# Expert passes of 32 tokens: u rows by slot, v rows by token, summed in four column strips

## The reference, cut to what matters

```
q = (tb @ w_q).reshape(blk, 8 heads, 2 halves, 128)
s = einsum('thsk,hsnk->thsn', q, sub_keys)            # 128 scores per head and half
sv, si = top_k(s, 16)                                 # 16 best of each half
cand = sv[:, :, 0, :, None] + sv[:, :, 1, None, :]    # 256 pairs, 16 best of them
idx = si0 * 128 + si1 ; g = softmax(best 16)
act = gelu(einsum('thkd,td->thk', u_emb[idx], tb))    # 128 experts per token (8 heads x 16)
out = einsum('thk,thkd->td', g * act, v_emb[idx])
```

## Time and profile before

| | |
|---|---|
| three timed runs | 2709.21, 2710.64 (median), 2720.2 us |
| profiled execution | 2708.6 us, span 2706.6 us |
| granted PE clock, mean | 0.908 of full speed |
| busy: PE, DVE, POOL, ACT | 79%, 65%, 40%, 24% |
| DMA queue 0 (POOL's) | 570.46 MB, 52.7% of 16 engines |
| first gather, third gather, last gather | 1160.45, 1171.86, 2680.22 us |

### The profile page before, as it was taken

How to read it: one execution, slowest core, us unless ns; L and a number is a source line. 1 busy time by engine, 2 the same in 40 slices (tenths; PEclk the granted TensorE clock), 3 DMA queues, 4 the chain that set the end, 5 groups by cost and what they waited for, 6 DMA issues and landing times.

```text
span 2706.6 us, 34195 instructions
## 1 busy us (share of the span) xinstructions
PE 2130.6 (79%) x9927; PEld 1409.1 (52%) x9927; DVE 1767.8 (65%) x4439; ACT 657.1 (24%) x1597; POOL 1091.2 (40%) x822
## 2 busy tenths in 40 slices
PE   6988899999988898986777677766776676668776
PEld 6987778889977898952222223222322222223222
DVE  5887721143288434158787778777877787778785
ACT  4334300132255224321111111111111111111112
POOL 2553224365433342344444344434443443344342
PEclk9999967799998999999989898989989998898898
DMA  3220023222311232279999999999999999899997
GB/s 140 80 77 1 1 79 139 102 77 86 109 63 47 75 113 71 85 296 391 407 363 362 363 412 360 371 371 396 362 364 372 401 373 359 355 400 360 374 381 287
DMA packets 101508, 664.75 MB, mean 246 GB/s; under 512 B 11744, under 2 KB 12000, under 8 KB 29056
## 3 DMA queue, kind: packets, MB, share of 16 engines
q0 software_dynamic: 78336, 570.46, 52.7%
q1 hardware_dynamic: 20160, 71.92, 7.9%
q10 hardware_dynamic: 2880, 20.97, 2.0%
HBM read 650.38 MB, written 12.14 MB: 245 GB/s over the span
## 4 chain that ended last, share of the span: by engine, by line
DVE 33%; PE 25%; issue 24%; DMA 10%; POOL 4%; ACT 3%; DVEq 1%; POOLq 0%; SPq 0%; ACTq 0%
PE ps L404 12%; DMA s_r<-in_uv,s_gidx 9%; DVE s_r L1768 7%; PE ps L788 5%; DVE s_r L1380 4%; POOL s_r_rounded L1178 3%; DVE s_h L1768 2%; PE ps L641 2%; ACT s_gth L1134 1%; DVE s_r L1712 1%; PE ps L653 1%; DVE s_g L1773 1%; DVE s_g L1776 1%; DVE s_g L1772 1%; DVE s_g L1774 1%
## 5 line engine op out<-in xcount | busy, mean ns | idle before, releaser
L788 PE MATMUL ps<-s_r 128*128 128x512 f32 x1632 | 789.4, 632 | 236.5 <-ACT s_r L1141 235.6
L404 PE MATMUL ps<-s_r_rounded 128*128 128x272 f32 x5760 | 766.9, 296 | 35.7 <-POOL s_r_rounded L1178 10.6
L404 PEld LDWEIGHTS ps<-s_r_rounded 128*128 128x128 f32 x5760 | 753.4, 195 | 46.5 <-issue 28.2
L1331 POOL DMA_INDIRECT s_r<-in_uv,s_gidx x408 | 488.9, 1198 | 531.3 <-PE ps L788 441.5
L788 PEld LDWEIGHTS ps<-s_r 128*128 128x128 f32 x1632 | 309.6, 199 | 709.5 <-ACT s_r L1141 388.0
L1768 DVE CUSTOM_DVE_ANT_0 s_r<-s_r 128x1024 f32<-128x1024 f32 x408 | 486.9, 1222 | 59.6 <-DMA s_r<-in_uv,s_gidx 56.6
L1178 POOL TENSOR_TENSOR s_r_rounded<-s_r,s_r_rounded 128x1024 fp32r<-128x1024 f32 x120 | 305.5, 2547 | 469.6 <-ACT s_r_rounded L815 469.6
L788 PE MATMUL ps<-s_h,s_r 128*128 128x512 f32 x544 | 298.0, 698 | 208.6 <-ACT s_r L1141 208.6
L788 PEld LDWEIGHTS ps<-s_h,s_r 128*128 128x128 f32 x544 | 115.7, 224 | 385.9 <-ACT s_r L1141 252.2
L1134 ACT ACTIVATE s_gth<-s_g 128x2 f32<-128x2 f32 x272 | 55.4, 204 | 1036.8 <-DVE s_g L1774 1036.8
L1331 POOL DMA_INDIRECT s_h<-in_uv,s_gidx x136 | 156.1, 1148 | 344.5 <-PE ps L788 320.5
(11 more groups left out here) (242 smaller groups left out, 1932.2 us busy)
## 6 DMA issues: line engine op xcount, KB each, us to landing
s_r<-in_wstream SPq DMA_DIRECT2D x120, 512.0 KB, 3.3
s_h<-in_sample_h_in ACTq DMA_DIRECT2D x8, 1024.0 KB, 5.0
out_sample_h_out<-s_h ACTq DMA_DIRECT2D x8, 1024.0 KB, 3.9
s_r<-in_uv,s_gidx POOLq DMA_INDIRECT x408, 10.2
s_r<-in_x SPq DMA_DIRECT2D x4, 544.0 KB, 6.8
s_r<-in_x SPq DMA_DIRECT2D x1, 2176.0 KB, 8.4
s_h<-in_uv,s_gidx POOLq DMA_INDIRECT x136, 9.0
out_y_prompt<-s_r SPq DMA_DIRECT2D x4, 512.0 KB, 9.9
```

The lines of the kernel that those rows point to most:

```text
L404: last = pe.matmul(ps[:, 2 * p + h, 0:HALF], fr(wp[:, k, :]), fr(xp[:, k, h * HALF:(h + 1) * HALF]), start=start and k == 0 and t == 0, st ...
L788: last = pe.matmul(ps[:, h, :], diag[:, s % 4, :], ring[s % RING][:, D_MODEL + 512 * h:D_MODEL + 512 * (h + 1)], start=s == 0, stop=s == S ...
L1331: pool.indirect_dma_start(ring[sl % RING], None, a["uv"], bass.IndirectOffsetOnAxis(ap=gidx[:, j, s:s + 1], axis=0)).then_inc(gath[sl % RI ...
```

## The change

The expert part is laid out anew, and its hardware loops are gone.

- The table is split into `u` and `v`, each with rows of 4 KB. A pass (17 of them) now takes 32 tokens and all eight heads: the tokens stand four times on the partitions, once for each pair of heads, so partition 32q + t is token t with heads 2q and 2q + 1. The last pass is that of the sample tokens, and no longer a special case.
- u rows are gathered by slot (32 gathers of 128 rows, 512 KB each). v rows are gathered by token: the 32 x 32 blocks of the index tile are transposed, so that one gather brings the 128 v rows of one token (32 gathers of 512 KB). Each kind has a ring of 8 tiles of 4 KB per partition. POOL issues v of pass g and u of pass g + 1 in turns.
- gelu and the slot weights are computed once per pass on 128 x 32 elements. The weights are transposed and copied into every 32nd column of a zeroed tile `ZB`, so that the stationary operand of token t is 32 columns wide with only column t filled.
- PE takes v rows in groups of four tokens. Each of the four goes to another strip of 32 output columns; ACT copies the four partial sums out (`empty`), and PE adds them with the constant `sel` (`total`). v ring slots come free four at a time.
- The queries are ordered so that four units give one score set, which PE computes at once for all passes with 32-column matmuls (`scores`, 68 matmuls, four times). DVE's second routing of pass 0 needs the last of them.
- SP copies the token rows of each pass four times into a double buffer `tbg`.

```diff
-            def gathers(it, j):
-                pool.wait_ge(idx_ready, it * 2 + (j + 1))
...
-                        pool.wait_ge(slot_free, it * SLOTS + (sl - RING + 1))
-
-                        pool.nop(nofuse=True)
-                    pool.indirect_dma_start(ring[sl % RING], None, a["uv"],
-                                            bass.IndirectOffsetOnAxis(ap=gidx[:, j, s:s + 1], axis=0)
-                                            ).then_inc(gath[sl % RING], 16)
+            pool.wait_ge(unit_done, U_WQ)
+            pool.memset(ZB, 0.0).then_inc(zb_set, 1)
+
+            def gather_u(g, s):
+
+                n = g * SLOTS + s
+                if s % TOPK == 0:
+                    pool.wait_ge(idx_ready, 2 * g + s // TOPK + 1)
+                if n == 2:
+                    pool.wait_ge(unit_done, UNITS)
+                if n >= RING:
+                    pool.wait_ge(u_free, n - RING + 1)
+                pool.nop(nofuse=True)
+                pool.indirect_dma_start(uring[n % RING], None, a["u"],
+                                        bass.IndirectOffsetOnAxis(ap=gidx[:, g % 2, s:s + 1], axis=0)
+                                        ).then_inc(u_in[n % RING], 16)
+
+            def gather_v(g, t):
+
+                n = g * GT + t
+                if t == 0:
+                    pool.wait_ge(idxT_ready, g + 1)
+                if n >= RING:
+                    pool.wait_ge(v_free, (n - RING) // 4 + 1)
+                pool.nop(nofuse=True)
+                pool.indirect_dma_start(vring[n % RING], None, a["v"],
+                                        bass.IndirectOffsetOnAxis(ap=gidxT[:, g % 3, t:t + 1], axis=0)
+                                        ).then_inc(v_in[n % RING], 16)
...
-            gathers(0, 0)
-            gathers(0, 1)
-            with pool.Fori(1, ITERS) as it:
-                gathers(it, 0)
-                gathers(it, 1)
+            for s in range(SLOTS):
+                gather_u(0, s)
+            for g in range(GROUPS):
+                for t in range(GT):
+                    gather_v(g, t)
+                    if g + 1 < GROUPS:
+                        gather_u(g + 1, t)
...
+            def values(g):
+
+                bank = 4 * (g % 2)
+                pe.wait_ge(w_ready, g + 1)
+                if g >= 2:
+                    pe.wait_ge(evac_done, g - 1)
+                for quad in range(GT // 4):
+                    if g and quad == 3:
+                        total(g - 1)
+                    for c in range(4):
+                        n = g * GT + quad * 4 + c
+                        pe.wait_ge(v_in[n % RING], (n // RING + 1) * 16)
                     for h in range(2):
...
+                        for c in range(4):
+                            t = quad * 4 + c
+                            last = pe.matmul(ps[GT * c:GT * (c + 1), bank + h, :], ZB[:, g % 2, 31 * t + 31:31 * t + 63],
+                                             vring[(g * GT + t) % RING][:, 512 * h:512 * (h + 1)],
+                                             start=quad == 0, stop=quad == GT // 4 - 1)
+                    last.then_inc(v_free, 1)
...
+            def dot(g, s):
+
+                n = g * SLOTS + s
+                dve.wait_ge(u_in[n % RING], (n // RING + 1) * 16)
+                u = uring[n % RING]
+                dve.tensor_tensor_reduce(out=u, in0=u, in1=tbg[:, g % 2, :], scale=1.0, scalar=0.0, op0=ALU.mult,
+                                         op1=ALU.add, accum_out=act_z[:, s:s + 1]).then_inc(u_free, 1)
...
+            for g in range(GROUPS):
+                dve.wait_ge(tb_full[g % 2], 64 * (g // 2 + 1))
+                for s in range(SLOTS):
+                    if g + 1 < GROUPS:
+                        for j in range(2):
+                            if s == 11 * j + 2:
+                                route_keys(g + 1, j, 0)
...
+                    dot(g, s)
+                slot_weights(g)
```

More of the change, by code:

```diff
@@ L743, in _ @@
             pe.wait_ge(ld_late, 32)
[L745 to L761, removed]
+            def scores(i):
+                pe.wait_ge(q_ready, 4 * (i + 1))
+                if i:
+                    pe.wait_ge(sc_ready, i)
+                for g in range(GROUPS):
+                    for q in range(4):
+                        hs = (2 * q + i // 2) * 2 + i % 2
+                        out = ps[GT * q:GT * (q + 1), 4 + g // 4, (g % 4) * NKEYS:(g % 4 + 1) * NKEYS] if g < GROUPS - 1 \
+                            else ps[GT * q:GT * (q + 1), i, 512 - NKEYS:512]
+                        last = pe.matmul(out, qs[:, q, GT * g:GT * (g + 1)], keys[:, hs, :], start=True, stop=True)
+                last.then_inc(sc_mm, 1)
@@ L793, in _ @@
-            experts(0)
-            with pe.Fori(1, ITERS) as it:
-                experts(it)
-            pe.wait_ge(flushed, ITERS)
-            for h in range(2):
-                last = pe.matmul(ps[0:DEC, 2 + h, :], cc("sel"), X2T[:, TILES - 1, 512 * h:512 * (h + 1)],
-                                 start=True, stop=True)
-            last.then_inc(fin_mm, 1)
+            for i in range(HS // RINGW):
+                for j in range(RINGW):
+                    n = i * RINGW + j
+                    if n >= 2:
+                        pe.wait_ge(q_ready, n - 1)
+                    unit(U_WQ + n, j, j % 2, hn_parts, blocks=(hn_ready, KT) if n == 0 else None)
+                    if i and j == 0:
+                        scores(i - 1)
@@ L804, in _ @@
+            pe.wait_ge(sc_ready, 5)
+            for g in range(GROUPS):
+                values(g)
+            total(GROUPS - 1)
         @block.scalar
@@ L1158, in _ @@
-            squares = SC[:, 0:2, :].rearrange("p a b -> p (a b)")
-            softmax_exp(1)
-            experts(0)
-            with act.Fori(1, ITERS - 1) as it:
-                experts(it)
-            experts(ITERS - 1, True)
-            act.wait_ge(flushed, ITERS + 1)
-            token_norms(NCH, TILES, TILES, squares)
+            for n in range(HS):
+                keep_query(n)
+                if n >= RINGW and n % RINGW == 1:
+                    keep_scores(n // RINGW - 1)
+                if n == 2 * RINGW + 3:
+                    softmax_exp(0)
@@ new lines, in gelu_tanh @@
+            def gelu_tanh(g):
+                act.wait_ge(gl_in, g + 1)
+                act.activation(gth[:], g3[:], ACT.Tanh, scale=GELU_S).then_inc(gl_th, 1)
+            softmax_exp(1)
+            for g in range(GROUPS):
+                if g + 1 < GROUPS:
+                    softmax_exp(2 * g + 2)
+                if g >= 2:
+                    empty(g - 2)
+                if g + 1 < GROUPS:
+                    softmax_exp(2 * g + 3)
+                if g >= 5 and g % 4 == 1:
+                    token_norm((g - 5) // 4)
+                gelu_tanh(g)
```

359 lines of the change are left out of this document (152 added, 207 removed).

## The result

The changed kernel takes 2779.41 us (median of 4 runs, 2770.43 to 2799.22); the kernel before takes 2709.93 beside it. The ratio is 1.026, with an interval of 1.020 to 1.032: slower, by 0.6 of what was predicted (4.2%). The profiled execution took 2781.3 us with a span of 2779.5.

The account below looks back on a forecast made before the run. Experts were read as DMA-bound, with POOL bounding after the change: first dot 1187, pass 0 to 1237, 16 x 95.3 to 2762, last pass to 2805, ending at span 2823; predicted 2825 us (4.2% slower), range 2665 to 2930.

Parts of the forecast that it names:

- the choice on which all hung: POOL, experts: a gather of half the bytes still costs 0.94 us; if cost went with bytes, low end 49 us.
- the mean of a gather: POOL, experts: 1.19 us plus 0.30 between two, so 64 gathers cost 95.3 us a pass.
- bounds on both sides: POOL's pass: 79.7 us with DVE never in the way, 109 us at the high end.
- The last pass: End of the experts: 32 v gathers alone, 40 + 3 = 43 us.
- the loop of v buffers: Wait for v slots: landing 4.2 us plus 2.0 on PE, hidden behind eight issues of 11.9 us; costs nothing.
- The front end: Before the experts' passes: score sets 5 us each, first dot at 1187 against 1176.69, 10 us lost; first pass 50 us.
- the rivals, the first: Experts: DMA sets the pace as POOL's cost per gather falls; 87 us a pass, 2680 us; chance 0.19.
- DMA's share: Experts: DMA engines' share forecast near 0.85, at 350 GB/s.
- The forecast's own range: Whole kernel: POOL at 91 to 100 us a pass, 2765 to 2890 us; chance 0.59.
- Rival 2: Experts: 4 KB rows cost DMA the loose stretch's 48.1 ns per KB, 101 + 1.3 us a pass, 2935; chance 0.12.
- rival 3: Experts: PE becomes the bound, strips not overlapping and clock falling; 115 us a pass, 3155 us; chance 0.05.
- the turn of the loop: Old expert loop: DVE's 5.68 us standstill goes 15 times, 85 us in all, but off the path once POOL sets the pace.

Follow-up runs that it names:

- shorter holds: Changed kernel with each dot taken over 128 columns for 1024, same gathers and bytes: 2671.64 us (one run), 86.12 us a pass.
- short dots: Changed kernel with 2 KB rows gathered for 4 KB and dots over 128 columns, both together: 2573.36 us (one run), 80.98 us a pass.

## Why the prediction came out as it did

Direction and mechanism were right, and each stands on an experiment of its own.

POOL sets the pace: shown by half the bytes, which did not help, and by shorter holds, which did. That a half-size gather costs POOL the same 0.94 us was the choice on which all hung: shown, down to rows of 2 KB (0.961 us in the mean with short dots). The split alone makes an iteration of the old kernel 5 us longer, though there waits for PE have a part in it.

The term that was mis-sized is the mean of a gather, 1.19 us forecast and 1.121 measured (1.128 in the 16 passes). It makes a pass 91.7 us and not 95.3; 0.4 us of waits for buffers, which I had at nothing, come on top. So a pass was 92.08, and 16 passes 51 us less than forecast. The argument was that the share of gathers that meet a dot would stay. It did: 61% of the gathers took under 0.97 us before, 59% now. But how much of the dot is left when they meet it did not: 0.246 us over 0.94 in the mean then, 0.181 now. A gather that starts when a slot comes free and one that starts 0.30 us behind the last fall differently into the dots, and the half-row kernel (1.182) and the split one (1.086) show that this moves by itself. I had bounds on both sides and took the old mean; the rows of before hold nothing that gives 1.12.

The last pass went the other way: 43 us forecast, 54.4 measured. I had put the loop of v buffers at 4.2 us of landing and 2.0 of PE, against eight issues. In that pass there are no u gathers between, so four issues are 5 us; landing was 6.4; and a group took PE 3.64 us, on the lower clock level that I had named only as the other case. The groups then follow 7 us apart:

```profile
2709.34 3.64 PE L810 MATMUL ps<-s_r 128*32 128x512 f32 x16 [7.89 <-DMA s_r<-in_v,s_gidxT]
...
2715.91 3.64 PE L810 MATMUL ps<-s_r 128*32 128x512 f32 x16 [2.93 <-DMA s_r<-in_v,s_gidxT]
...
2723.68 3.64 PE L810 MATMUL ps<-s_r 128*32 128x512 f32 x16 [4.13 <-DMA s_r<-in_v,s_gidxT]
```

With the token rows in PSUM the last pass took 56.5 us, and 44.8 with 16 buffers, so the ring was the cause. This error and that of the gathers' mean have opposite signs, and the forecast came 11 us nearer by it.

The front end was close. Score sets took 3.92 us for 5, the first dot started at 1180.79 for 1187, and the first pass went its 50 us and a little (1232.4 for 1237):

```profile
1164.39 3.92 PE L768 MATMUL ps<-s_r 128*32 128x128 f32 x136 [0.71 <-ACT s_r L1115]
...
1180.79 1.19 DVE L1777 CUSTOM_DVE_ANT_0 s_h<-s_h 128x1024 f32<-128x1024 f32 x1
```

Together: -5 (pass stage starts earlier), -51 (passes), +11 (last pass), +1 (end), -44 of 2823 to 2779.5.

Of the rivals, the first had its floor right: once the holds are gone a pass is 86.1 us, and I had put DMA at 86 to 87. It was never reached in the changed kernel, where POOL's pace stood 6 us above it; and that pace is only 2.5 us above the 89.55 of the kernel before, which is why the change cost so little. What I had wrong was DMA's share, 0.85 forecast and 0.99 seen. The 0.85 did not even follow from my own terms, 87 us of DMA in a pass of 95.3, which are 0.91. The rest is the shorter pass, and that I took the full queue's ns per kilobyte for one that is not full (42.7 for 41.0). The forecast's own range was not its sum either: 91 and 100 us a pass give 2756 and 2900 us, and not 2765 and 2890. Rival 2 did not happen, rival 3 neither: 16 matmul records of 1.04 us pass in 3.64, so the four strips run side by side.

And the turn of the loop, 5.68 us, was never worth 5.68: in the old kernel itself its removal brings 2.4 us an iteration.

## What to carry to other kernels

Count the gathers of a gather-bound kernel, not only its bytes: an indirect DMA costs its issuing engine the same whether it brings 2, 4 or 8 KB a row. Where that engine sets the pace, look at what VectorE reads and copies beside it, and put one operand of long products in PSUM; where it doesn't, the same edit is worth nothing, so ask first who has idle time. And take a DMA share near 1 as a limit only after more bytes have been refused at it.

## What the runs showed that I had not expected

- With half the bytes the kernel ran slower, 95.80 for 92.08 us a pass.
- A copy from SBUF to SBUF on VectorE holds a gather as a dot does, with its one input: seven of seven gathers beside the 0.69 us copy of `tb` ended 0.80 to 0.81 us behind it.
- DMA engines at a share of 0.99 moved 367 GB/s, and at 1.02 moved 397 and 401 with the same rows: 42.7, 40.9 and 40.3 ns per kilobyte and engine.
- Two fp32 matmuls of full width a pass among column strips went with releases mostly 4.8 to 5.5 us behind the matmuls before them in 58 and 61% of the cases read, and cost 180 us against the same work in eight matmuls of 32 columns (2808.04 and 2628.04 us).
